# Last merge of the recurrences' triangular inverses in 64 by 64 by 64 products

## What is computed

```python
    lower = jnp.where(strict, jnp.einsum('bhncd,bhnsd->bhncs', kb, k) * decay, 0.0)
    rhs = jnp.concatenate([v * beta[..., None], kb * jnp.exp(g)[..., None]], axis=-1)
    sol = lax.linalg.triangular_solve(jnp.eye(C, dtype=jnp.float32) + lower, rhs,
                                      left_side=True, lower=True, unit_diagonal=True)
```

```python
        sa = jnp.einsum('bhij,bhj->bhi', S, at)
        S = S * wt[:, :, None, :] + sa[..., None] * bt[:, :, None, :] + vt[..., None] * kt[:, :, None, :]
```

## Time and profile before

| | |
|---|---|
| median of 3 runs | 3637.8 us (3635.0 to 3641.57) |
| the profiled execution | 3639.07 us |
| its span, first to last instruction | 3637.2 us |
| mean granted TensorE clock | 0.968 of full |
| PE busy | 3456.0 us, 95% of the span |
| DVE, ACT, POOL busy | 1612.1, 1246.4, 1238.6 us |
| recurrences of the first layer, merges and steps | about 695 to 814 us |
| of the second layer | about 1901 to 2019 us |

### The profile page before, as it was taken

The page is one execution under the profiler, slowest core; times in us unless marked ns, Lnnn a source line. Parts: engine busy times, 40 slices in busy tenths (PEclk is TensorE's granted clock), DMA queues, the critical chain, the costliest instruction groups (busy, mean ns, idle before and its releaser), DMA issues.

```text
span 3637.2 us, 45927 instructions
## 1 busy us (share of the span) xinstructions
PE 3456.0 (95%) x17032; PEld 2850.8 (78%) x17032; DVE 1612.1 (44%) x2740; ACT 1246.4 (34%) x1873; POOL 1238.6 (34%) x522
## 2 busy tenths in 40 slices
PE   7999998799999999999868999999799999999999
PEld 6888775688888888887658788877687888888887
DVE  5541488756431333147776543224564221253220
ACT  3222335434222422233543332223433332333321
POOL 3444331003444444443200244433302444434443
PEclk9999998699999999999879999999999999999999
DMA  4443221003443344322100144322201222212222
GB/s 172 144 144 106 85 76 47 13 1 105 150 140 121 121 146 144 118 91 76 53 24 1 67 147 145 133 99 76 70 1 53 98 98 98 81 64 96 95 98 92
DMA packets 100316, 335.22 MB, mean 92 GB/s; under 512 B 10800, under 2 KB 16592, under 8 KB 100064
## 3 DMA queue, kind: packets, MB, share of 16 engines
q1 hardware_dynamic: 83920, 277.83, 22.3%
q10 hardware_dynamic: 16272, 55.65, 4.4%
HBM read 330.78 MB, written 2.65 MB: 92 GB/s over the span
## 4 chain that ended last, share of the span: by engine, by line
issue 66%; POOL 23%; PE 10%; POOLq 1%; DVE 0%
POOL w_lo L640 23%; PE ps L2117 3%; PE ps L2115 3%; PE ps L2116 3%; POOLq L639 0%; POOLq L648 0%; PE ps L2136 0%; PE ps L2137 0%; PE ps L2141 0%; POOL table_hi L661 0%; POOLq L640 0%; POOL table_lo L661 0%; DVE x L1416 0%; POOLq L657 0%; POOLq L3133 0%
## 5 line engine op out<-in xcount | busy, mean ns | idle before, releaser
L640 POOL TENSOR_TENSOR w_lo<-w_raw,w_hi 128x1024 fp32r<-128x1024 f32 x510 | 1231.8, 2417 | 2374.7 <-ACT w_hi L683 2374.5
L2115 PE MATMUL ps<-h_hi,w_hi 128*128 128x512 f32 x2624 | 1032.2, 393 | 0.9 <-ACT mem L885 0.9
L2117 PE MATMUL ps<-h_hi,w_lo 128*128 128x512 f32 x2624 | 1022.3, 390 | 0.0
L2116 PE MATMUL ps<-h_lo,w_hi 128*128 128x512 f32 x2624 | 1022.2, 390 | 0.0
L683 ACT ACTIVATE w_hi<-w_raw 128x1024 fp32r<-128x1024 f32 x510 | 538.5, 1057 | 917.9 <-DMA w_raw<-in_tiles 917.6
L2115 PEld LDWEIGHTS ps<-h_hi,w_hi 128*128 128x128 f32 x2624 | 493.2, 188 | 118.1 <-issue 14.3
L2116 PEld LDWEIGHTS ps<-h_lo,w_hi 128*128 128x128 f32 x2624 | 493.3, 188 | 104.5 <-issue 3.4
L2117 PEld LDWEIGHTS ps<-h_hi,w_lo 128*128 128x128 f32 x2624 | 493.2, 188 | 103.3
L1385 DVE TENSOR_TENSOR a_lo<-sil,a_hi 128x512 f32 (+1 forms) x132 | 300.2, 2274 | 498.6 <-ACT a_hi L825 498.6
L2116 PE MATMUL ps<-a_lo,w_hi 128*128 (+1 forms) x1120 | 435.7, 389 | 0.0
L2115 PE MATMUL ps<-a_hi,w_hi 128*128 (+1 forms) x1056 | 410.8, 389 | 0.0
(11 more groups left out here) (469 smaller groups left out, 3710.1 us busy)
## 6 DMA issues: line engine op xcount, KB each, us to landing
w_raw<-in_tiles SPq DMA_DIRECT2D x510, 512.0 KB, 3.3
ada_raw<-in_ada_tiles ACTq DMA_DIRECT2D x96, 512.0 KB, 3.3
x<-in_x_t SPq DMA_DIRECT2D x2, 1024.0 KB, 6.5
sq<-in_cond ACTq DMA_DIRECT2D x4, 512.0 KB, 4.2
mem<-gates SPq DMA_DIRECT2D x8, 256.0 KB, 4.1
out_t<-x SPq DMA_DIRECT2D x1, 2048.0 KB, 7.1
consts<-in_consts SPq DMA_DIRECT2D x1, 1280.0 KB, 12.8
core_mem<-gates SPq DMA_DIRECT2D x8, 128.0 KB, 2.9
```

Source lines behind the costliest of these rows:

```text
L640: nc.gpsimd.tensor_tensor(w_lo[:, s, :], w_raw[:, s, :], w_hi[:, s, :].bitcast(F32), ALU.subtract).then_inc(S["w_lo_ready"], 1)
L2115: nc.tensor.matmul(bank, wh, hi, start=first, stop=False, skip_group_check=True)
L2116: nc.tensor.matmul(bank, wh, lo, start=False, stop=False, skip_group_check=True)
L2117: return nc.tensor.matmul(bank, wl, hi, start=False, stop=last, skip_group_check=True)
```

## The change

At level 6 the products leave out the rows and columns that are zero or unused. `lower_products` takes rows 0 to 63 and columns 64 to 127 of the matrix as its stationary operand and the upper left block of the inverse as the moving one, and writes partitions 64 to 127 of the bank alone. ACT copies those 64 partitions. `inverse_products` takes rows 64 to 127 of that copy and the lower right block of the transposed inverse. The number of instructions and their order stay; levels 4 and 5 stay.

```diff
                     for g in range(2):
                         act.wait_ge(S["t1_ready"], merge_turn(b, lev, g) + 1)
-                        nc.scalar.activation(core_mem[:, C_T1 + g, 0:w], ps[:, 2 + g, 0:w], ACT.Copy).then_inc(S["t1_out"], 1)
+                        rows = slice(HD if lev == 6 else 0, P)
+                        nc.scalar.activation(core_mem[rows, C_T1 + g, 0:w], ps[rows, 2 + g, 0:w], ACT.Copy).then_inc(S["t1_out"], 1)
...
                     for h in range(4):
                         inv = inv_units(n)[:, g, blk(h)]
+                        lower = lower_units(n)[:, g, blk(h)]
+                        out = ps[:, 2 + g, HD * h:HD * h + HD]
                         if lev == 4:
                             ins = nc.tensor.matmul(ps[:, 2 + g, blk(h)], cm[:, C_N + g, blk(h)], inv, start=True, stop=True)
-                        else:
-                            ins = nc.tensor.matmul(compact(ps[:, 2 + g, HD * h:HD * h + HD], lev), lower_units(n)[:, g, blk(h)], evens(inv, lev), start=True, stop=True)
+                        if lev == 5:
+                            ins = nc.tensor.matmul(compact(out, lev), lower, evens(inv, lev), start=True, stop=True)
+                        if lev == 6:
+                            ins = nc.tensor.matmul(out[HD:P], lower[0:HD, HD:P], inv[0:HD, 0:HD], start=True, stop=True)
                     ins.then_inc(S["t1_ready"], 1)
...
                         rows = slice(0, P if lev == 4 else HD)
-                        out = compact(ps[rows, 4 + g, HALF + HD * h:HALF + HD * h + HD], lev)
-                        ins = nc.tensor.matmul(out, t1(h), odds(inv_t(h), lev), start=True, stop=True)
+                        out = ps[rows, 4 + g, HALF + HD * h:HALF + HD * h + HD]
+                        if lev == 6:
+                            ins = nc.tensor.matmul(out, t1(h)[HD:P], inv_t(h)[HD:P, HD:P], start=True, stop=True)
+                        else:
+                            ins = nc.tensor.matmul(compact(out, lev), t1(h), odds(inv_t(h), lev), start=True, stop=True)
                     ins.then_inc(S["dx_ready"], 1)
```

## The result

| | before | changed |
|---|---|---|
| median of the comparison, 5 runs each | 3637.52 us (3634.98 to 3641.57) | 3654.07 us (3652.35 to 3659.97) |
| the profiled execution | 3639.07 us | 3652.35 us |
| its span | 3637.2 us | 3650.4 us |
| mean granted TensorE clock | 0.968 | 0.964 |

The ratio of the changed kernel to the one before is 1.0051 (95% interval 1.004 to 1.0061): slower by 16.5 us. Forecast was 3635.6 us, no change, with a range up to 3641. The result lies 13 us above the range.

A forecast was written before the change was run, and what follows sets the result against it. PE, busy 95% of the span, was taken as the bound. Gains of 1.4 us (steps 2 and 3, both layers) and 0.8 us (step 0, first layer) sum to 2.2: 3637.8 to 3635.6 us, no change, range 3631 to 3641.

The forecast's parts named there:

- The bound and the cover: PE, busy 95% of the span, bounds the kernel; at some places in the recurrences waits for ACT or DVE absorb savings.
- Group 0's gain: Steps 1 to 3, first products: 0.42 us saved only lengthens the idle before group 1 from 0.16 to about 0.58.
- The wait for the state in step 1: DVE bounds the end of step 1: PE's wait grows from 1.38 to 1.7 us, gain 0 in both layers.
- step 0 of the second layer: Gain 0, since PE's 6.23 us wait for DVE covers it; without that cover 0.8 us.
- The terms of the sum: 1.4 us from steps 2 and 3 of both layers plus 0.8 from the first layer's step 0: 2.2 us.
- First products: Level 6, 64 columns loaded in place of 128: group 1 gains 0.34 us per PE-bound step, 1.4 us in four.
- Step 0 of the first layer: At half clock, smaller level-6 products let PE restart earlier until DVE holds it: 0.8 us gained.
- Second products: Level 6, 64 columns already and only depth halved: no gain, sixteen records still about 1.07 us; at most 0.53 per step.
- The change of shape: Extra array-shape switch between first products and `writes`: costs 0.08 us; wrong if `writes` starts over 0.7 us after group 1.
- The rows: Load time follows columns, not rows, so halving the rows of level 6's products gives no time.
- rival B: Clock falls at the start of step 2 behind step 1's longer idle, costing 10.6 us: 3646.2 us, slower; chance 0.05.
- The last line of the prediction: Wrong on the whole if step 2 shortens over 1 us, or granted clock is 0.5 anywhere in steps 2 to 3.

The follow-up runs named there:

- e6: Changed kernel plus one 128*128 matmul on constants in the idle before group 1 of level 6's first products: 3642.1 us, ratio 1.0008.
- e7: Kernel before with first products 128*64 over all rows, plus one 128*128 matmul on constants before group 1: 3640.3 us, ratio 1.0010.
- e9: Changed kernel plus one 64 by 64 matmul on constants in the idle before group 1: 3640.5 us, ratio 1.0009.
- e13: Kernel before with first products 128*64 over all rows and second products 64*64: 3642.6 us, ratio 1.0012.
- e12_again: The changed kernel measured once more under a new label, in a later batch: 3653.8 us, ratio 1.0042 to the kernel before.
- e2_rows: Kernel before with level 6's first products over 64 rows but all 128 columns, second products unchanged: 3645.6 us, ratio 1.0018.
- e15_between: Changed kernel with half of `writes` moved between the two groups of level 6's first products: 3637.2 us, ratio 0.9993.
- e16_between_before: Kernel before with half of `writes` moved between the two groups of level 6's first products: 3640.7 us, ratio 1.0005.
- e1: Kernel before with level 6's first products narrowed to 64 columns over all 128 rows, and the changed ACT copy: 3641.2 us, ratio 1.0008.
- e5: Kernel before with one extra ACT copy ahead of group 1 to lengthen PE's idle, products unchanged: 3644.7 us, ratio 1.0024.
- e3: Kernel before with only level 6's first products made 64*64, second products unchanged: 3644.9 us, ratio 1.0021.
- e14: Kernel before with one extra ACT copy ahead of group 1 and the second products made 64*64: 3643.9 us, ratio 1.0016.

## Why the prediction failed

**The bound and the cover** were read rightly. Group 0's gain became idle: 0.16 to 0.59 us, "about 0.58" forecast. The wait for the state in step 1 went from 1.38 to 1.66, "1.7" forecast. DVE held step 0 of the second layer, 23.66 and 23.73 us.

**The terms of the sum** were right wherever the clock was the one that they were worked out for. First products: 0.34 us per PE-bound step forecast; steps 2 and 3 measure 0.26 to 0.30 less at full clock (25.90 against 26.18, 24.66 against 24.95, in e6, e7, e9 and e13), four such steps 1.1 us, not 1.4. Step 0 of the first layer, at half clock: 0.8 forecast, 27.20 - 26.33 = 0.87 in e12_again, the one of the two executions of the changed kernel in which that step stood at half clock. Second products: 0 forecast, 1.07 us before and after. The change of shape: line 2620 starts 0.61 us behind group 1, under the 0.7 that I had set as the mark. The rows gave nothing: 1.03 us for eight records in e2_rows. Two small slips did not matter: by its own numbers the second products of step 0 end 1.4 us earlier, not 1.5, and the highest run of before, 3641.57, is just outside the range.

**The step that failed is the one that put the idle before group 1 and the quarter-array products at nothing.** The prediction has "the idle of 0.16 us becomes about 0.58 and nothing is gained": the idle was entered as harmless, because nothing waits behind it in time, and the halved rows were taken for a term without gain or price. The sum had no term for the clock. What the runs showed in its place is a fall to 1.2 GHz in the last merges of steps 2 and 3, which made these steps 4.43 and 2.84 us longer in each layer.

The clock stood only in rival B, at a chance of 0.05, and there in one place: the start of step 2, behind the idle of step 1, with the answer that the wide grams follow at once. There nothing fell at the 1.66 us of idle that the change left; it fell at 2.19 us (e15_between) and once at 1.74 (e16_between_before), for 1.6 us. The fall that decided comes some 18 us later, in the last merge, for which rival B had half a sentence, "has PE do its last merge in a quarter of the array", and no price. The change made the idle before group 1 there almost four times as long and halved the rows on both sides of it. The price was mis-sized as well: rival B had one fall, of 10.6 us; there are four, and longer steps 4 on top (+2.6 and +0.7), less 1.4 us in steps 0 and 1 of the first layer. The result stands 8 us above rival B's 3646.2. The last line of the prediction, that it is wrong if the clock is 0.5 anywhere between the start of step 2 and the end of step 3, named the right place to look.

**What I should have weighed**: the earlier trace rows already showed PE busy for 4.00 of 4.00 us at 0.50, in a stretch of level-6 products and level-5 merges. I used it as an argument that a fall may last. It says more: this kind of work, even without a gap, did not bring the clock back up in step 0 of the first layer, where it had fallen before PE began:

```profile
695.10:721.30 26.20, 26.20 (x138) 0.50 0.00 1
```

So the clock was to be priced wherever the change touched such work.

What the runs settle: the loss is in the clock and in no wait. Without the idle (e6, e9, e15) steps 2 and 3 hold the clock, with the changed products left in; with full rows and narrow columns (e1, e7, e13) they hold it too. Halved rows alone (e2, +0.18%) and idle alone (e5, +0.24%) each bring a third to a half of the loss. Counted over the last merges of steps 1 to 3 in both layers, six in each profile, the clock fell in four in the changed kernel, e12_again and e2, in three in e5, in two in e3, in one each in e1 and e14, and in none in the others.

What stays open: how much of the 16.5 us is due to rows and how much to idle, since the parts don't add, and the falls come in one step of one execution and another of the next; and why e1, e6, e7, e9 and e13 are still 2.5 to 6 us above the kernel before. Part of that is in step 4, whose length goes with its clock: 12.4 us at 1.00, 15.5 at 0.78, 17.4 at 0.65, 18.1 at 0.62. Both layers' steps 4 together have 4.4 of e6's 5.9 us and 3.9 of e13's 4.4, but only 0.3 to 1.8 us in e1, e7 and e9. No instruction of step 4 differs there, and e16, with the products of before, has 17.42 and 12.40 us, so it isn't shown that the change causes the longer ones, the 3.3 us of the changed kernel included.

## What to carry to other kernels

On a kernel that PE bounds, a change which makes PE's work smaller has two prices: the time of the instructions, and the clock of everything behind them. A gain that only turns into idle in a stretch of small matmuls need not be free; fill it with work that the kernel has anyway (here half of `writes`, some 16 us), and cut a product's columns before its rows, since here only the columns gave time. Idle that can't be filled with own work may be worth matmuls on constants: 6.8 us here on the kernel before, 12 to 14 together with the narrower products (0.4%), with no product changed in value.

## What I had not expected of the hardware

- Behind an idle of 0.6 to 0.9 us, or behind 16 records per step on half the rows, the granted clock went from 1.00 to 0.50 for 3 to 10 us (0.54 and 0.50 from 761.5 to 771.5 in the changed kernel), with PE busy all that time.
- Longer idles often left the clock at 1.00: 0.91 us ahead of narrow full-row products (eleven of twelve merges in e1_columns and e13_columns_second), 1.66 us ahead of the grams (changed kernel), 1.76 us there in the first layer of e16_between_before. 1.74 us in its second layer and 2.19 us in e15_between did not. The length of one gap alone doesn't tell.
- Step 0 of the first layer takes 23.55 or 26.33 us in two executions of the same changed kernel, by the clock in it; single steps of the two profiles differ by up to 3.1 us, while the medians agree to 0.3 us. One execution's table of steps shows a mechanism, and its size must come from the medians.
